# Output projections of the first and the last block computed by chunks of 128 features, and the seventh gate unit merged ahead of the head normalization

## The reference

```
merged = sum(sigmoid(gates) * branch_out)        # block 1: RWKV-7, stick-breaking, memory attention
x1 = x  + merged @ w_out                         # wo
x2 = x1 + conv_ffn(x1)
x3 = x2 + mlstm_mixer(x2)                        # its output projection is aw
x4 = x3 + conv_ffn_2(x3)
x5 = x4 + moba_attention(x4) @ w_o               # bo
out = x5 + conv_ffn_2(x5)
```

## Time and profile before

| | |
|---|---|
| median of 3 runs | 1174.16 us (1172.38 to 1175.66) |
| profiled execution | 1175.13 us, span of its instructions 1173.3 us |
| TensorE busy | 98% of the span |
| VectorE, ScalarE, GpSimd busy | 79%, 59%, 28% |
| mean granted TensorE clock | 0.999 |

### The profile page before, as it was taken

The page is one execution under the profiler, slowest core; times in us unless marked ns, Lnnn a source line. Parts: engine busy times, 40 slices in busy tenths (PEclk is TensorE's granted clock), DMA queues, the critical chain, the costliest instruction groups (busy, mean ns, idle before and its releaser), DMA issues.

```text
span 1173.3 us, 23286 instructions
## 1 busy us (share of the span) xinstructions
PE 1154.2 (98%) x9212; PEld 1062.2 (91%) x9212; DVE 931.8 (79%) x1345; ACT 694.5 (59%) x1075; POOL 329.9 (28%) x252
## 2 busy tenths in 40 slices
PE   9999999999999999999999999999999999999998
PEld 8988778878899999889888999998898789999987
DVE  5989774458889999866758799997676858999963
ACT  6787854446656666644557576664455666666642
POOL 2334111000013555312102245551146123555500
PEclk9999999999999999999999999999999999999999
DMA  8744211226556555555432555555554325555552
GB/s 309 236 150 143 92 37 48 83 91 213 183 183 213 182 183 189 176 188 179 161 127 91 185 183 184 185 181 179 187 173 144 127 77 176 185 187 183 180 182 87
DMA packets 55012, 189.01 MB, mean 161 GB/s; under 512 B 6144, under 2 KB 7296, under 8 KB 54656
## 3 DMA queue, kind: packets, MB, share of 16 engines
q1 hardware_dynamic: 53312, 182.48, 47.0%
q10 hardware_dynamic: 1600, 5.12, 1.3%
HBM read 186.52 MB, written 1.05 MB: 160 GB/s over the span
## 4 chain that ended last, share of the span: by engine, by line
PE 54%; DVE 35%; issue 6%; ACT 4%; DMA 1%; SPq 0%; DVEq 0%; ACTq 0%
PE psA L485 43%; DVE rounded L1915 17%; DVE arena L1918 13%; PE psB L485 10%; DVE arena L1915 2%; ACT rounded L1252 2%; ACT arena L1252 1%; ACT L1252 1%; DMA arena<-in_w 1%; DVE arena L2325 0%; DVE rounded L1918 0%; PE psB L795 0%; PE psB L1184 0%; PE psB L778 0%; DVE arena L1956 0%
## 5 line engine op out<-in xcount | busy, mean ns | idle before, releaser
L485 PE MATMUL psA<-rounded,rounded 128*128 128x256 f32 (+1 forms) x7236 | 1006.1, 300 | 7.9 <-DVE rounded L1915 6.9
L485 PEld LDWEIGHTS psA<-rounded,rounded 128*128 128x128 f32 x7236 | 941.9, 191 | 64.8 <-issue 9.5
L1915 DVE TENSOR_TENSOR rounded<-arena,rounded 128x1024 fp32r<-128x1024 f32 (+2 forms) x364 | 477.0, 1342 | 68.1 <-ACT rounded L1252 65.3
L1252 ACT ACTIVATE rounded<-arena 128x1024 fp32r<-128x1024 f32 (+2 forms) x508 | 414.8, 857 | 174.3 <-DVE arena L2284 61.9
L1747 POOL TENSOR_TENSOR arena<-arena 128x256 f32<-128x256 f32 (+1 forms) x113 | 178.2, 1582 | 557.9 <-ACT arena L1252 206.7
L1252 ACT ACTIVATE arena<-arena 128x256 f32<-128x256 f32 (+7 forms) x297 | 155.5, 555 | 175.7 <-DVE arena L2349 109.6
L1918 DVE SCALAR_TENSOR_TENSOR arena<-arena 128x255 f32<-128x255 f32 (+4 forms) x338 | 190.6, 606 | 12.5 <-ACT arena L1252 9.9
L485 PE MATMUL psB<-arena 64*64 64x64 f32 (+9 forms) x1464 | 136.7, 285 | 4.8 <-issue 2.8
L485 PEld LDWEIGHTS psB<-arena 64*64 64x64 f32 (+4 forms) x1464 | 94.0, 152 | 35.0 <-issue 23.6
L1915 DVE TENSOR_TENSOR arena<-arena,psA 128x256 f32<-128x256 f32 (+1 forms) x101 | 45.5, 450 | 50.3 <-PE psA L485 39.9
L1832 POOL TENSOR_TENSOR rounded<-arena,rounded 128x256 fp32r<-128x256 f32 x63 | 72.0, 1144 | 33.9 <-ACT rounded L1252 33.9
(11 more groups left out here) (75 smaller groups left out, 182.1 us busy)
## 6 DMA issues: line engine op xcount, KB each, us to landing
arena<-in_w SPq DMA_DIRECT2D x343, 512.0 KB, 3.5
arena<-in_mem ACTq DMA_DIRECT2D x2, 512.0 KB, 7.9
arena<-in_x ACTq DMA_DIRECT2D x1, 1024.0 KB, 4.9
arena<-in_con ACTq DMA_DIRECT2D x1, 1024.0 KB, 8.0
out<-arena SPq DMA_DIRECT2D x8, 128.0 KB, 3.4
arena<-in_con ACTq DMA_DIRECT2D x1, 992.0 KB, 5.7
arena<-in_w SPq DMA_DIRECT2D x2, 256.0 KB, 3.2
arena<-in_x SPq DMA_DIRECT2D x2, 256.0 KB, 6.0
```

The lines of the kernel that those rows point to most:

```text
L485: ins_ = nc.tensor.matmul(o, l, r, start=start, stop=stop, skip_group_check=shared)
L1252: return nc.scalar.activation(o, i, f, **kw)
L1915: return V.tensor_tensor(o, a, b, op)
```

## The change

`wo` and `bo` become 8 units of one chunk each (8 blocks, one slot), computed by `mm_sum`: the first two by a new `sum_first`, the others by `project_sum`. VectorE takes them with `residual_sum`, ScalarE's `gained` handles one chunk per unit, and GpSimd's squares wait for two counts. In the gate units, unit 6 and the conversion of slots 13 and 14 are put ahead of the logarithms (ScalarE) and of the head's multiplications (VectorE), and these multiplications behind unit 8, their rest behind unit 11. In the mLSTM block a slot is converted behind `hr_rest(1)` instead of ahead of it, and for `aw` one slot is rounded and converted earlier at its third unit.

```diff
+            def sum_first(names, src, wait):
+                o = [open_(name) for name in names]
+                assert state["blk"] == 0
+                w = [[], []]
+                for m in range(2):
+                    w[m] = [weights(1) for k in range(KD)]
+                    if m:
+                        state["inc"] = False
+                    for k in range(6):
+                        if m == 0:
+                            ready(pe, wait, k + 1)
+                        mm_sum(o[m], w[m][k], src, k, k == 0, False)
+                for m in range(2):
+                    for k in range(6, KD):
+                        if m == 0:
+                            ready(pe, wait, k + 1)
+                        elif k == 6:
+                            state["inc"] = True
+                        last = mm_sum(o[m], w[m][k], src, k, False, k == KD - 1)
+                    close(last, names[m])
...
-            project_first("wo0", (mgH, mg), "merged_rest")
-            project([f"wo{u}" for u in range(1, 4)], (mgH, mg))
+            sum_first(("wo0", "wo1"), (mgH, mg), "merged_rest")
+            project_sum([f"wo{m}" for m in range(2, KD)], (mgH, mg))
...
-                    split_to(SLOT_END[name] + (4 if name == "aw1" else 2))
+                    split_to(SLOT_END[name] + {"aw1": 4, "aw2": 3}.get(name, 2))
...
             split_to(SLOT_END["br%d.%d" % BR[6]] + 2)
+            gate_of(6)
+            split_to(SLOT_END["br%d.%d" % BR[7]] + 3)
             for u in range(2):
                 release(A(YQ[:, 2 * u:2 * u + 2, :], take(f"var{u}")[:, :], ACT.Ln, bias=epsln,
                           scale=1.0 / 64), f"var{u}")
-            split_to(SLOT_END["br%d.%d" % BR[7]] + 1)
             act.wait_ge(*freed("var0"))
             act.wait_ge(*freed("var1"))
             A(YQ, YQ, ACT.Exp, scale=-0.5).then_inc(sem("y_inv"), 1)
-            gate_of(6)
...
             for u in range(USUM, 3 * KD):
                 merge(u)
-                if u == 9:
-                    for h in range(2):
...
+                if u == 8:
+                    head_scaled()
+                elif u == 11:
+                    head_rest()
...
-            residual([f"wo{u}" for u in range(4)], "x1", "f0", "n2")
+            residual_sum([f"wo{m}" for m in range(KD)], "x1", "f0", "n2")
...
-            split_to(L0 + 11)
+            split_to(L0 + 10)
...
             hr_rest(1)
+            split_to(L0 + 11)
...
-            residual([f"aw{u}" for u in range(4)], "x3", "f1", "f0", (1, 1, 0, 0))
+            residual([f"aw{u}" for u in range(4)], "x3", "f1", "f0", (1, 1, 1, 0))
...
-            residual([f"bo{u}" for u in range(4)], "x5", "f2", "f1")
+            residual_sum([f"bo{m}" for m in range(KD)], "x5", "f2", "f1")
```

More of the change, by code:

```diff
@@ L130 @@
        "mk0", "mk1", "mv0", "mv1"] + [g + f"br{m}.{n}" for u, (m, n) in enumerate(BR) for g in (("",) if u < USUM else ("g", ""))]
-       + [f"wo{u}" for u in range(4)] + ffn_units(0)
+       + [f"wo{m}" for m in range(KD)] + ffn_units(0)
        + ["lq0", "lq1", "lk0", "lk1", "lv00", "lv01", "lv10", "lv11", "lo0", "lo1", "lo2", "lo3"]
@@ L134 @@
        + [f"bq{u}" for u in range(4)] + [f"bk{u}" for u in range(4)] + ["bv00", "bv01", "bv10", "bv11"]
-       + [f"as{h}" for h in range(8)] + [f"bo{u}" for u in range(4)] + ffn_units(2))
+       + [f"as{h}" for h in range(8)] + [f"bo{m}" for m in range(KD)] + ffn_units(2))
 def slot_ends():
@@ L142, in slot_ends @@
         token = n in ("sv0", "sv1", "mv0", "mv1") or n[:2] in ("lv", "bv")
-        blocks += KD if n.startswith("gbr") else W4 if "g" + n in LIN else 12 if n.startswith("br") else KF if n.startswith("down") else 2 * KD
+        blocks += KD if n[:3] == "gbr" or n[:2] in ("wo", "bo") else W4 if "g" + n in LIN else 12 if n.startswith("br") else KF if n.startswith("down") else 2 * KD
         ends[n] = -(-blocks // SLOT)
@@ L1202, in _ @@
                     scores(h + 3)
-            project_first("bo0", (aoH, ao), "ao_rest")
-            project([f"bo{u}" for u in range(1, 4)], (aoH, ao))
+            sum_first(("bo0", "bo1"), (aoH, ao), "ao_rest")
+            project_sum([f"bo{m}" for m in range(2, KD)], (aoH, ao))
             ffn(2, "r6")
@@ L1530, in _ @@
             A(YQ, YQ, ACT.Exp, scale=-0.5).then_inc(sem("y_inv"), 1)
-            gate_of(6)
             for u in range(USUM, 3 * KD):
                 gate_of(u)
-                if u == 8:
+                if u == 10:
                     for h in range(2):
@@ L1544, in ffn @@
             def ffn(f, rms_, g, xready):
-                gained(f"f{f}", g, [xready[0] + str(u) for u in range(4)], xready[1])
+                gained(f"f{f}", g, [xready[0] + str(u) for u in range(4 if f == 1 else KD)], xready[1])
                 if f == 0:
@@ L1820, in ffn @@
             def ffn(f, x):
-                squares(f"f{f}", x)
+                squares(f"f{f}", x, 1 if f == 1 else 2)
                 def up(i, j):
@@ L2243, in _ @@
                 if q < 3:
-                    split_to(SLOT_END["br%d.%d" % BR[q + 3]] + (2, 2, 1)[q])
+                    split_to(SLOT_END["br%d.%d" % BR[q + 3]] + (2, 1, 1)[q])
             for u in range(2):
@@ L2249, in _, with head_scaled, head_rest @@
             split_to(SLOT_END["br%d.%d" % BR[6]] + 2)
[L2250 to L2261, removed]
-            merge(6)
+            merge(6)
+            split_to(SLOT_END["br%d.%d" % BR[7]] + 3)
+            def head_scaled():
+                ready(dve, "y_sq", 2)
+                mark(tt(YT, YT, GT, ALU.mult))
+                settle()
+                ready(dve, "y_inv")
+                for u in range(2):
+                    c = slice(2 * u, 2 * u + 2)
+                    mark(tt(YT[:, c, :], YT[:, c, :], YQ[:, c, :], ALU.mult))
+                settle()
+                for u in range(2):
+                    c = slice(2 * u, 2 * u + 2)
+                    tt(ys[:, c, :], YT[:, c, :], BN[:, c, :], ALU.add).then_inc(sem("ys"), 1)
+            def head_rest():
+                for u in range(2):
+                    c = slice(2 * u, 2 * u + 2)
+                    ready(dve, "ys_upper", 3 + u)
+                    tt(fr(ys[:, c, :]), ys[:, c, :], rd(YH[:, c, :]), ALU.subtract).then_inc(sem("ys_split"), 1)
             def merged_rest(m):
```

3 lines of the change are left out of this document (removed).

## The result

The changed kernel takes 1189.93 us (median of 4 runs, 1189.06 to 1192.17) beside 1173.61 us of the kernel before (4 runs, 1172.38 to 1175.66). The ratio is 1.0144, 95% interval 1.0132 to 1.0157: slower by 16.3 us, where 17.1 were forecast on the median shown (1174.16 to 1191.3). The profiled execution took 1189.06 us, with a span of 1187.3.

What follows compares the result with a forecast made beforehand. TensorE, busy 98% of the span, was taken as the bound. The profiled 1175.13 + 16.2 (projections) + 0.9 (head) + 0 (mLSTM, `aw`) gave 1192.2, or 1191.3 us as median; range 1188 to 1194.5, 1184 to 1198 with rivals 2 to 4.

Steps and rivals of the forecast that it cites:

- The bound and the chunk cycle: `wo` and `bo`: VectorE's serial steps, 3.67 or 4.56 us a chunk against TensorE's 2.83, set the pace; 7.5 us lost in `bo`.
- the table: Step-by-step start times of chunks 2 to 7 and FFN unit 0's slots in a projection, from its first matmul.
- GpSimd's part: `wo` and `bo`: GpSimd's square additions lengthen VectorE's cycle for chunks 3 and 5; without them together +12, not +16.2 us.
- Rival 4: `wo` and `bo`: GpSimd hinders less, its additions falling beside ScalarE's part; +12 instead of +16.2, 1187 us; 8%.
- The later reciprocal: Behind `bo` and likewise `wo`: the reciprocal comes 3.1 us behind the unit's end, not 2.5; TensorE's wait grows by 0.6.
- The streams: `wo` and `bo`: matmuls of 512 and 256 columns instead of three of 256 save 0.9 us over 2 x 64 pairs.
- The head: Gate units: the wait moves from slot 13 to slot 16, 3.0 us, with the slow clock behind it; +0.9 us.
- Rival 2: Head: the wait disappears because slot 16 is converted by 269.9; saves 4.0 us instead of costing 0.9, 1186.4 us; 10%.
- mLSTM and `aw`: Slots converted earlier at `aw` and later behind `hr_rest(1)`: waits only move, so 0; bound -1.1 us.
- Rival 3: `wo` and `bo`: their waits bring the slow clock, 2.8 to 5.6 us in all, 1194 to 1197 us; 14%.
- Rival 1: `wo` and `bo`: VectorE overlaps a chunk's steps within 2.83 us; 1174.2 us, 6%; head's wait gone too, 1169.3, another 4%.

Runs made afterwards that it cites:

- e3: Changed kernel, but in `wo` and `bo` ScalarE rounds slot m+3 ahead of chunk m's copy and VectorE converts it between chunk m's memset and subtraction; 1174.85 us.
- e4: Changed kernel without GpSimd's additions of the squares behind `wo` and `bo`, a one-column memset in their place; 1185.85 us.
- e2: Changed kernel with the two projections put back as before, all other edits kept; 1174.44 us, ratio 1.001 to the kernel before.
- e1: Kernel before with only the two projections `wo` and `bo` changed; 1190.15 us, ratio 1.0139 to the kernel before.
- e8: Changed kernel, but in `wo` and `bo` ScalarE rounds slot m+3 ahead of chunk m's copy, VectorE's order unchanged; 1184.82 us.
- e5: Changed kernel with slot 16 converted ahead of the head's five operations instead of behind them; 1190.68 us.
- e7: Kernel before with only (2, 2, 1) made (2, 1, 1), the slots converted behind each state; 1173.64 us, ratio 0.9998.
- e10: Changed kernel with the projections of before, the head's product ahead of unit 7 and its other six operations one each behind units 9 to 14; 1170.66 us.

## Why the prediction was right

**The bound and the chunk cycle: right.** VectorE, hidden before, sets the pace. 3.67 and 4.56 us were read off the down projection; 3.66 and 4.54 came. The last addition stands 361.63 - 334.23 = 27.40 us behind the first; the table had 32.7 - 5.2 = 27.5. The unit ends after 36.4 us, measured 36.38. The table's starts hold one by one: for 9.0, 12.6, 16.3, 20.9, 24.5, 29.1 and 32.8 `bo` has 9.04, 12.70, 16.36, 20.91, 24.58, 29.07 and 32.68 us. A cycle from another place with the same sequence of steps and the same neighbours was worth more than any sum of durations. e3 shows the cause: the same work, interlocked otherwise, 15 us less.

**GpSimd's part: right.** 12 instead of 16.2 without it was the bound; e4 gave back 4.1 by the medians, 3.4 of it seen in the two projections. Rival 4 (its additions fall beside ScalarE's part) was false, since the addition follows GpSimd's multiplication and so falls on the conversion.

**The later reciprocal: 0.6, measured 0.42 and 0.5.** TensorE's wait grew from 0.17 to 0.53 and 0.52, and the start of the FFN behind the sum of squares took another 0.27 that no row of before shows: 366.41 - 365.47 = 0.94 in place of 359.49 - 358.82 = 0.67. That is 0.6 for each projection. What gives the rest back between there and the next norm was not looked at, and 0.42 and 0.5 are smaller than what the same stretches differ by between executions.

**The streams: mis-sized.** 0.45 us a projection was the term. In e3, where nothing waits, the 64 pairs of `bo` take 22.70 us, 0.3547 each, and 22.99 before: 0.29, so about 0.6 for both projections, between the 0.9 of the sum and the 0.3 that the prediction set beside it. With the FFN's first unit it is 0.11, since the 48 matmuls of that unit take 6.06 us in place of 5.88; why was not followed up. It changed nothing here, since the waits took it.

**The head: mechanism right, size +0.9, measured +1.3** (e2, and 114.31 - 113.02 between the changed kernel and e1). The wait at slot 13 gone, one at slot 16 of 2.78 us instead of 3.0, the clock at half behind it. What was wrong is what stands behind the wait: 1.4 us for the clock as a cost of its own, and no wait after it, so that with the full clock the head would have gained 0.5. e8 has the same head and the full clock throughout:

```profile
270.68 3.01 PE L485 MATMUL psA<-rounded,rounded 128*128 128x512 f32 x16 [2.78 <-DVE rounded L1937]
274.34 8.75 PE L485 MATMUL psA<-rounded,rounded 128*128 128x512 f32 x48 [0.66 <-DVE rounded L1937]
283.68 16.52 PE L485 MATMUL psA<-rounded,rounded 128*128 128x512 f32 x92 [0.59 <-DVE rounded L1937]
```

Two more waits for VectorE take its place, and the 408 matmuls of the gate units last 77.95 us against 77.92. VectorE delivers the slots no sooner; a slow TensorE only hides its own waiting. Rival 2 (the wait disappears) was false, and e5 shows that moving slot 16 alone would not have made it true. How the 1.3 splits between the longer wait and the rest was not separated, and it is not exact: the 408 matmuls last 76.64, 76.61 and 76.61 us with the old order (before, e1, e7) and 77.92, 77.94, 78.00 and 77.95 with the new one (the changed kernel, e2, e3, e8), but 77.09 in e4, with the same instructions up to there and the slow clock. One slip in the working: a vanished wait would have brought 277.1 - 3.0 - 1.4 - 276.20 = -3.5 us by the prediction's own steps, where it has -4.0; nothing here turns on it.

**mLSTM and `aw`: 0, measured 0** (-0.05 us from the start of `aw`'s row to its sum of squares). At `aw` the edit moves the waits and not what the last one hangs on. The mLSTM block ahead of it takes 86.59 us before and 86.60 after, with the same wait of 0.27 and 0.28 us in it.

**Missing: (2, 1, 1).** The prediction passed over this edit; it is worth -0.6 to -0.7 us by the traces of e7 and before. With +7.6 and +7.6 for the projections, +0.9 for what follows them, +1.3 and -0.6 the sum is +16.8, against 16.3 measured. The forecast of +17.1 had two terms of opposite sign off, the head by 0.4 and this edit by 0.6. That they nearly cancel is luck; the 16.2 of the projections, against 15.2 + 0.9 here, is not.

**Rival 3, a slow clock in the projections: false.** Seven waits a projection, up to 1.49 us, and the only slow stretch ahead of the program's end is the one at the head. Rival 1 (VectorE overlaps the steps by itself) was false; e3 is what it would have looked like.

## What to carry to other kernels

When a residual or an eviction is cut into smaller units, the fixed waits between engines (here 0.58 and 0.47 us for ScalarE) are paid per unit: read the whole cycle of a unit from a place that has the same sequence, and compare it with TensorE's time for that unit before counting what the streams save. If an engine must wait for another inside the cycle, put work there that is due anyway, as the next slot's conversion in e3. Work in one piece (the head) is better given out in parts that fit the slack of a unit than put behind or ahead of one slot: e5 moved a wait, e10 cut it from 2.78 to 0.49 us.

## What the runs showed of the hardware

The half clock does not follow from the length of a wait alone. A wait of 2.78 us was followed by it in the changed kernel and not in e8, with the same instructions up to there; this is the window of e8 that stands beside the changed kernel's at 0.50:

```profile
271.00:273.00 2.00, 2.00 (x13) 1.78 (x12) 1.24 (x3) 2.00 (x4) 0.00 (x0) 1.00 0.29 51
```

In e3, with a wait of 2.83 us until 270.47, the clock was still at half in the window from 273 to 276 (in the changed kernel 0.93 from 274 to 276), and TensorE was busy throughout:

```profile
273.00:276.00 3.00, 3.00 (x11) 2.62 (x10) 2.97 (x5) 2.10 (x6) 0.00 (x0) 0.50 0.57 182
```

Waits of 1.61 and 1.74 us with eight matmuls between them (e5) brought none. The Trainium skill, "TensorE: Matmul & The Clock Gate", section "What's actually happening", says that the phase of the gate's window against the kernel varies from run to run. The difference between the changed kernel and e8 fits that, but no row here shows the phase.

GpSimd and VectorE held each other up by whole instructions: a conversion ended 1.08 us behind GpSimd's addition whether it had begun 0.13 us into it (e8), 0.33 (the changed kernel) or 0.73 (`wo` in the trace before, 344.50 + 1.71 against 343.77 + 1.36), and a multiplication of GpSimd's took 1.96 instead of 1.04 us behind a conversion.

The same stream of matmuls did not always run at one pace. In the 8 us from 66 us behind the start of the gate units, with TensorE busy throughout and the clock at 1.00, the changed kernel ran 47 matmuls and e4, with the same instructions, 49. The cause is open, and it is one of the steps of about a microsecond between executions.
